# First feed-forward's down product as 7 block products, with its block sums on GpSimd and pair products accumulated in PSUM

## The reference

```
up = rms_norm(x, norm2_g) @ w_up                  # 1024 x 1024 times 1024 x 5632
up = causal_depthwise_conv(up, ffn_dw_w)          # 3 taps per channel
gate, val = split(up)                             # 2816 columns each
x = x + (silu(gate) * val) @ w_down               # 1024 x 2816 times 2816 x 1024
```

## Time and profile before

| | us |
|---|---|
| median of 3 runs (2778.55, 2779.89, 2785.9) | 2779.89 |
| the profiled execution, its own time | 2782.16 |
| its span | 2780.5 |
| PE busy in the span | 2714.4 (98%) |
| DVE busy | 1758.4 (63%) |
| ACT busy | 1131.0 (41%) |
| POOL busy | 640.6 (23%) |
| DMA, all queues | 414.45 MB |

### The profile page before, as it was taken

The page is one execution under the profiler, slowest core; times in us unless marked ns, Lnnn a source line. Parts: engine busy times, 40 slices in busy tenths (PEclk is TensorE's granted clock), DMA queues, the critical chain, the costliest instruction groups (busy, mean ns, idle before and its releaser), DMA issues.

```text
span 2780.5 us, 31459 instructions
## 1 busy us (share of the span) xinstructions
PE 2714.4 (98%) x12219; PEld 2197.0 (79%) x12219; DVE 1758.4 (63%) x2235; ACT 1131.0 (41%) x1590; POOL 640.6 (23%) x548
## 2 busy tenths in 40 slices
PE   9989999999999999999999999999999999999997
PEld 7877668788888788888878888766777888888886
DVE  6886554689999843243324444566548787776567
ACT  4423442343433443221235655665345322223543
POOL 1213111000110042010002222113423244444113
PEclk9999999999999999999999999999999999999999
DMA  3224532334444464344623232666543365657874
GB/s 123 84 83 140 145 80 103 140 104 122 130 121 121 157 234 138 117 150 157 214 84 102 69 99 85 173 183 189 195 169 125 137 213 188 204 189 248 262 251 133
DMA packets 147283, 414.45 MB, mean 149 GB/s; under 512 B 18616, under 2 KB 23352, under 8 KB 147136
## 3 DMA queue, kind: packets, MB, share of 16 engines
q1 hardware_dynamic: 115024, 309.97, 34.3%
q0 software_dynamic: 32112, 102.48, 11.9%
HBM read 309.46 MB, written 102.92 MB: 148 GB/s over the span
## 4 chain that ended last, share of the span: by engine, by line
PE 79%; DVE 12%; ACT 4%; issue 3%; DMA 2%; POOL 1%; SPq 0%; DVEq 0%; POOLq 0%; ACTq 0%
PE ps L218 77%; DVE cacc L189 3%; PE ps L221 2%; ACT PB L183 1%; POOL ga L186 1%; DVE cv L189 1%; DVE PB L189 1%; DVE tr L189 1%; DVE tl L186 0%; DVE YA L186 0%; DMA raw<-in_w_win 0%; DVE sqacc L186 0%; DVE ps L198 0%; DVE T L189 0%; DMA RBc<-scr_inv 0%
## 5 line engine op out<-in xcount | busy, mean ns | idle before, releaser
L218 PE MATMUL ps<-AH,wh 128*128 128x512 f32 (+1 forms) x1104 | 446.0, 404 | 19.4 <-DVE T L186 7.0
L218 PE MATMUL ps<-AH,wl 128*128 128x512 f32 (+1 forms) x1104 | 432.0, 391 | 0.0
L218 PE MATMUL ps<-AL,wh 128*128 128x512 f32 (+1 forms) x1104 | 431.6, 391 | 0.0
L218 PEld LDWEIGHTS ps<-AH,wh 128*128 128x128 f32 (+1 forms) x1104 | 206.6, 187 | 72.2 <-issue 10.4
L218 PE MATMUL ps<-stk,stk 128*128 128x512 f32 (+3 forms) x832 | 245.1, 409 | 12.8 <-DVE small L198 6.9
L218 PEld LDWEIGHTS ps<-AH,wl 128*128 128x128 f32 (+1 forms) x1104 | 206.5, 187 | 46.6
L218 PEld LDWEIGHTS ps<-AL,wh 128*128 128x128 f32 (+1 forms) x1104 | 207.0, 187 | 44.4 <-issue 2.9
L218 PEld LDWEIGHTS ps<-stk,stk 128*128 128x128 f32 x832 | 147.9, 191 | 83.2 <-issue 34.0
L186 DVE TENSOR_TENSOR wl<-raw,wh 128x1024 fp32r<-128x1024 f32 (+1 forms) x76 | 112.7, 1484 | 150.2 <-ACT wh L183 135.0
L218 PE MATMUL ps<-euh,ewt 128*128 128x512 f32 x640 | 198.8, 391 | 2.1 <-DVE eul L186 2.1
L186 POOL TENSOR_TENSOR wl<-raw,wh 128x1024 fp32r<-128x1024 f32 (+3 forms) x47 | 102.0, 2171 | 319.3 <-ACT wh L183 319.2
(11 more groups left out here) (324 smaller groups left out, 6373.6 us busy)
## 6 DMA issues: line engine op xcount, KB each, us to landing
ewr<-in_dn SPq DMA_DIRECT2D x88, 256.0 KB, 3.2
pwr<-in_w_up SPq DMA_DIRECT2D x38, 512.0 KB, 4.1
swr<-in_w_gu SPq DMA_DIRECT2D x38, 512.0 KB, 4.1
raw<-in_w_w2in SPq DMA_DIRECT2D x32, 512.0 KB, 4.2
scr_u<-cv SPq DMA_DIRECT2D x22, 512.0 KB, 2.6
eur<-scr_u SPq DMA_DIRECT2D x44, 256.0 KB, 3.4
scr_u<-uu SPq DMA_DIRECT2D x22, 512.0 KB, 8.6
alr<-in_dn POOLq DMA_DIRECT2D x11, 1024.0 KB, 9.9
```

The lines of the kernel that those rows point to most:

```text
L218: return Issued(self, self.e.matmul(out, l, r, start=start, stop=stop, skip_group_check=onto))
```

## The change

The three things that the diff does, with what each touches:

- **The down product** takes 7 block products of 11 steps (`NK` = 11, 77 steps; `DOWN1`). The first two products use raw weight blocks ("a") and raw input blocks ("b"), the others sums of weight blocks ("s", scratch `s_s1`) or input blocks ("t", scratch `s_t1`). Every step now loads its own input tile. Products 0, 2, 4 and 6 share one set of four banks (`d_bank`) and 2, 4 and 6 accumulate onto what is there; 1, 3 and 5 begin afresh in the other set. `evacuate(p, j)` runs once per product and bank, into one or two tiles of `XR` (`INTO1`).
- **The sums** are 22 jobs on POOL, `weight_sums(j)` and `block_sums(j)` in turn, through one buffer `TW1`: a load of 1 MB, four sums, a store of 1 MB, and each job waits for the store of the job before (`jd1`). Job n-1 stands between `added(n)` and `added(n+1)` in POOL's list; the last 4 follow after the pairs. `TW1` takes the room of input slots 20 and 21, so that `u_load(20)` waits for all jobs.
- **A pair's products** go to four banks in place of seven, alternating between two sets (`f1_bank`); the later products accumulate onto banks that ACT has copied out first (`taken`, `taken_shared`, `taken_fifth`). DVE loses `shared`, `shared_end` and part of `value` and `value_end`. ACT's copies are put between its `high` instructions for the next pair.

The core of the diff:

```
-    SHAPE1 = [("X11", 0), ("X21", 1), ("T2", 5), ("T1", 4), ("X22", 6), ("T3", 2), ("T4", 3)]
+    SHAPE1 = [("X11", 0), ("X21", 1), ("T2", 5), ("T1", 4), ("T3", 2), ("X22", 6), ("T4", 3)]
+    def f1_bank(self, n, x):
+        return self.bank(4 * ((n + 1) % 2) + x)
+    DOWN1 = [(("a", 0, 0), ("b", 0, 1)), (("a", 1, 0), ("b", 1, 1)), (("s", 0), ("t", 2)), (("s", 3), ("t", 1)),
+             (("s", 1), ("t", 0)), (("s", 2), ("b", 1, 0)), (("a", 1, 1), ("t", 3))]
+    INTO1 = [((0, 1),), ((0, 1),), ((0, 0),), ((0, 0), (4, 0)), ((4, 0),), ((0, 0),), ((4, 1),)]
...
     def pe_ff1: part(n, i), and the loop over pairs
-            out = self.s_bank(n, i)
+            out = self.f1_bank(n, (0, 2, 0, 1, 0, 1, 0)[i])
+            first, onto = i in (0, 1, 3), i not in (0, 1, 3)
...
+                if i == 0:
+                    q.wait_ge(S.uev, 2 * (PLAIN + n - 1) if n else 0)
+                elif i == 2:
+                    q.wait_ge(S.snp1, 3 * n + 1)
+                elif i == 4:
+                    q.wait_ge(S.snp1, 3 * n + 2)
+                elif i == 5:
+                    q.wait_ge(S.snp1, 3 * n + 3)
+                elif i == 6:
+                    q.wait_ge(S.ev1, 3 * n + 2)
                 part(n, i)
-        for w in range(88):
-            p, k = w // 22, w % 22
+        for w in range(7 * NK):
+            p, k = w // NK, w % NK
...
     def act_ff1: the loop over pairs
+            if n:
+                tap_gate(i)
+            tap_value(i)
             taken(n)
             if n:
-                silu(PLAIN + n - 1)
+                silu(i)
             if n + 1 < NQ:
-                for b in (0, 5, 4, 2):
-                    high(n + 1, b)
+                high(n + 1, 0)
+                high(n + 1, 4)
+            taken_shared(n)
+            if n + 1 < NQ:
+                high(n + 1, 5)
+            else:
+                d_high(0)
+                u_high(0)
+            taken_fifth(n)
+            if n + 1 < NQ:
+                high(n + 1, 2)
...
     def dve_ff1: the loop over pairs
             if n:
                 value_end(n - 1)
                 taps(0, i)
+                taps(1, i)
             gate(n)
-            if n:
-                taps(1, i)
-            shared(n)
             if n:
                 gated(i)
             if more:
                 s_sums(n + 1)
-            shared_end(n)
-            if more:
-                s_lows(n + 1, 0, 1)
-            gate_end(n)
-            if more:
-                s_lows(n + 1, 2)
+                s_lows(n + 1, 0, 2, 1)
...
             value(n)
+            value_scaled(n)
             if more:
                 s_lows(n + 1, 3)
...
+            gate_end(n)
...
+        for w in range(6, 7 * NK):
+            d_low(w)
+            u_low(w)
+            for p in range(5):
+                if 0 <= w - NK * (p + 1) - 7 < 4:
+                    evacuate(p, w - NK * (p + 1) - 7)
...
     def pool_ff1
+        def weight_sums(j):
+            q.wait_ge(S.tl1, 4)
+            q.wait_ge(S.jd1, 32 * j)
+            q.dma(self.TW1[:, :, :], self.io["dn1"][2 * j:2 * j + 2, :, :, :].rearrange("i h p c -> p (i h) c")).then_inc(
+                S.jl1, 16)
+            a11, a21, a12, a22 = [self.TW1[:, x, :] for x in range(4)]
+            q.wait_ge(S.jl1, 48 * j + 16)
+            q.tt(a22, a21, a22, ALU.add).then_inc(S.jb1)
...
+            q.dma(self.io["s_s1"][j, :, :, :], self.TW1[:, :, :]).then_inc(S.jd1, 16)
...
+        added(0)
+        for n in range(1, NQ):
             added(n)
-        q.wait_ge(S.dul1, 10)
-        for u in range(10, 22):
-            u_low(u)
...
+            job(n - 1)
+        for x in range(NQ - 1, 2 * NK):
+            job(x)
...
     def sp_ff1
         def u_load(u):
...
+            if u in (20, 21):
+                q.wait_ge(S.jd1, 32 * NK)
+            if kind == "t":
+                q.wait_ge(S.jd1, 32 * k + 32)
+                src = self.io["s_t1"][k, :, at[0], :]
...
-        for w in range(9, 88):
+        for w in range(9, 7 * NK):
             d_load(w)
-            if w < 21:
+            if w < 7 * NK - 1:
                 u_load(w + 1)
             if 12 <= w < 20:
                 q.wait_ge(S.prd1, 7 * NQ)
                 q.dma(self.XR[:, w - 12, :], self.io["s_x1"][w - 12, :, :]).then_inc(S.dxr, 16)
```

More of the change, by code:

```diff
@@ L381, in __init__ @@
         self.EU, self.EUR, self.EU_FREE = [], [], []
[L382 to L389, removed]
+        homes = [("g", k, 0, 1) for k in range(4)] + [("g", 4, 0, 2), ("g", 5, 0, 2), ("g", 4, 1, 6), ("g", 5, 1, 6)]
+        homes += [("a", k, 1, 7) for k in (0, 1, 2)] + [("a", 6, 1, 7), ("a", 7, 1, 7)]
+        homes += [("a", k, 1, 7) for k in (4, 5, 3)] + [("g", k, 1, 7) for k in range(4)]
         for which, k, half, free in homes:
@@ L395, in __init__ @@
             self.EU_FREE.append(free)
+        for x in range(2):
+            one = Area(nc, sq + 4096 * x, sq + 4096 * x + 4096)
+            self.EUR.append(Area(nc, one.lo + 2048, one.hi).get("eur", [P, 512])[:, :])
+            self.EU.append(tuple(one.get("eu", [P, 512], F32R)[:, :] for _ in range(2)))
+            self.EU_FREE.append(7)
+        self.TW1 = Area(nc, sq, sq + 8192).get("tw1", [P, 4, 512])
         w = Area(nc, lo + 4096, TOP)
@@ L1628, in part @@
                 xh, xl = self.sums1(name, k)
-                q.mm(out, h[:, ws], xh, k == 0, False)
-                q.mm(out, h[:, ws], xl, False, False)
-                t = q.mm(out, l[:, ws], xh, False, k == 3)
+                q.mm(out, h[:, ws], xh, first and k == 0, False, onto)
+                q.mm(out, h[:, ws], xl, False, False, onto)
+                t = q.mm(out, l[:, ws], xh, False, k == 3, onto)
             t.then_inc(S.prd1)
@@ L1742, in act_ff1 @@
         tap_value(1)
-        for b in (0, 5, 4, 2):
+        for b in (0, 4, 5, 2):
             high(0, b)
@@ L1791, in act_ff1 @@
-        for w in range(88):
-            if w >= 6:
-                d_high(w)
-            if 6 <= w < 22:
-                u_high(w)
-            if 30 <= w < 52:
-                u_high(w - 8)
-            for p in range(3):
-                if 0 <= w - 22 * (p + 1) - 8 < 4:
-                    n = 4 * (p % 2) + w - 22 * (p + 1) - 8
-                    square(p // 2, n)
-                    if p < 2:
-                        into(0, n)
+                for x in range(m):
+                    if x % 2 == m % 2 and x not in (0, 4):
+                        q.wait_ge(*self.added1(x))
@@ L1804, in act_ff1 @@
+                q.act(self.sqF[m % 2][:, :], self.XR[:, n, c], ACT.Square).then_inc(self.squared1(m)[0])
+        for w in range(6, 7 * NK):
+            d_high(w)
+            u_high(w)
+            if 52 <= w < 56:
+                square(w - 52)
+            if 63 <= w < 67:
+                square(4 + w - 63)
+                into(0, 4 + w - 63)
+            if 72 <= w < 76:
+                square(8 + w - 72)
+                into(0, w - 72)
         for n in range(4):
@@ L2072, in pool_ff1, with job @@
+        def job(x):
+            if x % 2:
+                block_sums(x // 2)
+            else:
+                weight_sums(x // 2)
+        added(0)
+        for n in range(1, NQ):
+            added(n)
+            job(n - 1)
+        for x in range(NQ - 1, 2 * NK):
+            job(x)
+        for m in (1, 2, 3, 5, 6, 7, 8, 9, 10, 11):
+            summed(m)
         for n in range(4):
@@ L2186, in ready @@
         def ready(k):
-            q.wait_ge(S.pl, 8 * half + k + 1)
+            q.wait_ge(S.pl, 8 + k + 1 if half else (k + 4) % 8 + 1)
         def norm(half, k):
```

295 lines of the change are left out of this document (161 added, 134 removed), and 4 rows, old and new, of the table SHARED.

## The result

| | before | after |
|---|---|---|
| median, us (runs) | 2779.22 (4) | 2893.20 (2882.05, 2892.39, 2894.02, 2894.18) |
| ratio of the runs, 95% interval | | 1.0396 [1.0366, 1.0427] |
| the profiled execution, its own time, us | 2782.16 | 2882.05 |
| its span, us | 2780.5 | 2880.3 |
| the 19 pairs, us | 362.41 | 473.99 |

The change makes the kernel 4% slower, 114 us from median to median; the forecast was 2835 us, 56 us slower, with 2880 as the end of the range. The profiled execution of after is the shortest of its four; its granted clock was 0.976 over the span, that of the others 0.973. What follows is told on it, trace against trace, where the difference is 99.8 us: 111.6 in the pairs, -12.4 in the down product, 0.6 around them.

What follows compares the result with a forecast made beforehand. PE was taken as the bound. 35.7 us gained, against some 58 us of waits in the pairs and 32 before step 19, put the down product's end 55.2 us later: 2837.4 for the profiled execution, 2835 us predicted, range 2794 to 2880.

Steps and rivals of the forecast that it cites:

- What is removed: Down product: 132 matmuls fewer (29.9 us) and about 5 us gained at its start; ends 35.7 us earlier if nothing new waited.
- The wait inside a pair: Fifth product waits for ACT's copy, behind a high part that waits for the adding DMAs: 2.7 us a pair.
- 0.2 us of hand-overs: In each pair, an estimated addition to ACT's 0.615 + 0.577 us between the adds' landing and PE's fifth product.
- Together 0 to 2.5 us; I take 0.5: Extra per pair for store queueing, lowered PE clock and slower DVE sums; brings a pair to 22.3 us (21.1 to 24.3).
- three unknowns: In each pair: adds queue behind a 1 MB store; PE's clock falls after the wait; DVE's sums take 0.795, not 0.692 us.
- up to 2 us: In each pair, the possible cost of PE's clock being lowered by a wait of 2.7 us.
- The chain of sums: POOL's 22 one-buffer jobs take 22.2 us each (19.9 to 25.3), holding up the pairs' adds; last store ends at 1075.2.
- The formula for the end: Down product ends at 585.1 + 22 s + 164.8, s being the jobs' mean spacing; equals the old end at s = 19.8 us.
- The stop before step 19: Down product: PE waits some 32 us for the last store, then step 20's input load, the last XR load and `evacuate(0, 0)`.
- the sums stay hidden: Rival: adds land within 9.5 us and jobs take no more than a pair; 2764 us, down to 2744; chance 0.10.
- only the landing counts: Rival: sums go as the shortest did and adds land early, s = 19.4 to 21.1; 2772 to 2809 us; chance 0.13.
- DVE and POOL hold each other up: Rival: two DVE sums a pair each wait for a POOL sum; pairs of 24.3 us, 2869 to 2903 us; chance 0.12.

Runs made afterwards that it cites:

- run 3: The changed kernel with 12 more matmuls into an unread bank, ahead of the fifth product's wait, in each of the first 18 pairs: 2840.53 us, ratio 1.0207.
- run 2: The changed kernel with one line moved: ACT's copy for the fifth product stands ahead of the high part of block 4: 2851.75 us, ratio 1.0252.
- run 1: The changed kernel without POOL's 22 jobs of block sums, raw blocks read in their place: 2836.97 us, ratio 1.0193.
- run 10: The changed kernel with reordered ACT and DVE lists, 16 input slots, POOL's jobs in halves, and five more orders on top: 2774.25 us, 0.9974 of the kernel before.

## Why the prediction was wrong in size

- **What is removed:** right. 35.7 us forecast, 35.6 measured without the jobs (244.99 to 209.44 us).
- **The wait inside a pair:** right in place, cause and length. The fifth product, released by ACT's copy, which waits behind the adds: 2.7 us forecast, 2.67 without the jobs and 2.71 with short transfers. (The 0.2 us of hand-overs in it do not show: in the pair shown PE starts 1.17 us after ACT's high part does, where 1.4 us from the landing were taken.)
- **The step that failed is "Together 0 to 2.5 us; I take 0.5".** It held three unknowns. The clock fell with 16 of 18 gaps and cost 2.06 us a pair, the whole of the "up to 2 us" that the prediction named; the reason given for 0.5 spoke of the sums and of the store, and not of the clock. The store cost 1.35 us a pair (4.02 - 2.67), by another way than the one named: it is the value load, on SP's queue, that lands later beside it, not the adds behind it on their own queue (from SP's issue to the adds' 6.1 us on average over 17 pairs, against 4.5 without the jobs; from there to DVE's sums 7.6, against 7.9). This is no price of the store as such: in run 3, where the store is issued 2.5 us behind the load, the load is not late. Why the two fall together in after, where the pairs are longer than the jobs, no run settles. DVE's sums cost nothing. Together 3.4 us, so that the bound of 2.5 was too small too. 18 pairs x (25.1 - 22.3) = 50 us, which is more than the 45 us by which the profiled execution (2882.05) missed the 2837.4 forecast for it; the shorter stop, below, gave some of it back. The other three executions of after were 10 to 12 us longer still, and of them only the lower granted clock is known (0.973).
- **The chain of sums:** the job was right (22.2 forecast, 22.1 where the clock did not fall), its part was not. The prediction had the pairs held up behind the jobs; with pairs of 25.1 us the jobs waited for the pairs (POOL 6 us a pair for the value load, 78.5 us over 13 pairs) and followed each other in 24.25 us. The formula for the end holds with that: 585.1 + 22 x 24.25 + 164.8 = 1283.4, measured 1285.5.
- **The stop before step 19:** right in place and in its chain. Its length was 16.3 us and not 32, since the longer pairs put PE's arrival off by more than the jobs: PE stopped at 1108.4 in place of 1050, and the last store had landed by 1118.2 in place of 1075.2.
- **The rivals:** "the sums stay hidden" and "only the landing counts" fall, by 16 of 18 gaps. "DVE and POOL hold each other up" had 2869 to 2903 us, and the median lies in it, but by luck: DVE's sums took 692 ns and the sixth product waited once, in the last pair. POOL's sums did slow DVE's low parts (1722 ns), which released no wait. The time alone would have picked the wrong rival; the rows of the wait decide.

## What to carry to other kernels

In a list that an engine works through in order, a copy that PE waits for must not stand behind an instruction that waits for a transfer: moving one line gave back 41 us here. Where a change puts a wait like these, of 2.5 us or more, into every round of a loop, price the fall of PE's clock in every round, at about the 1.7 to 2.1 us that it cost here, and not as a small chance. Sums on an engine that has time are not free either: their transfers can delay other queues' loads and their instructions hold DVE's up, so what runs beside them has to be looked at by order, not by busy time.

## What the runs showed that was not expected

- Adding 216 matmuls made the kernel 52.7 us faster (2893.20 to 2840.53): the clock stayed up over the gaps, which had cost 37 us in the pairs, and the value load was no longer late.
- Cutting the jobs' transfers to an eighth made the pairs longer, 481.8 us in place of 474.0, since POOL's sums then met DVE's.
- Of the gaps of after and of run 2, none under 2 us brought half clock, and every one from 3 us on did but one of 3.47; those between went both ways (in run 1 the clock stayed up behind a gap of 2.80 us that ended at 781.08, and fell behind one of 2.44 that ended at 757.33). In run 10 it fell behind one of 1.86 us.
- A store of 1 MB on POOL's queue, issued at about the same time, put the landing of a load on SP's queue off from 3.8 to 5.5 us (medians), and POOL's adds behind it by 3.5 us in the pair shown; issued 2.5 us behind the load, it did not (3.9 us).
